# RWKV projections on Trainium2: K's product moved to the head of each tile, the low-rank products behind it

## What is computed

```python
xx = token_shift(hn) - hn
xs = hn[None] + xx[None] * mu[:, None, None, :]
r, k, v, g = jnp.einsum('pbsd,pdf->pbsf', xs[:4], w_in)
xv, xw, xa = xs[2], xs[4], xs[5]
w_log = -jax.nn.softplus(-(w0 + jnp.tanh(xw @ w1) @ w2)) - 0.5
a = jax.nn.sigmoid(a0 + (xa @ a1) @ a2)
```

## Time and profile before

| | us |
|---|---|
| median of 3 runs | 4384.56 |
| lowest, highest | 4382.27, 4392.83 |
| profiled execution: its own time | 4379.64 |
| profiled execution: span | 4377.9 |
| TensorE busy | 4071.0 (93%) |
| VectorE, ScalarE busy | 1501.9 (34%), 1254.9 (29%) |
| granted TensorE clock, mean | 0.968 |

### The profile page before, as it was taken

How to read it: one execution, slowest core, us unless ns; L and a number is a source line. 1 busy time by engine, 2 the same in 40 slices (tenths; PEclk the granted TensorE clock), 3 DMA queues, 4 the chain that set the end, 5 groups by cost and what they waited for, 6 DMA issues and landing times. The chain is left out here.

```text
span 4377.9 us, 70847 instructions
## 1 busy us (share of the span) xinstructions
PE 4071.0 (93%) x30130; PEld 2388.2 (55%) x30130; DVE 1501.9 (34%) x3325; ACT 1254.9 (29%) x2197; POOL 320.8 (7%) x143
## 2 busy tenths in 40 slices
PE   8999999989899999998999998998999879889798
PEld 3458844445466666544554455444444378788343
DVE  3346611132144444112331053103322176766111
ACT  1147700022255555201220054112222222221132
POOL 0000000000000000000000000000000046654000
PEclk9999999999999999998999999999999999999899
DMA  5000042042400100202002011014111121110300
GB/s 208 20 23 2 2 173 82 5 127 75 151 23 23 45 23 23 82 10 106 14 10 96 15 40 58 0 38 164 48 48 48 71 81 53 59 65 28 144 19 19
DMA packets 162429, 254.03 MB, mean 58 GB/s; under 512 B 48500, under 2 KB 92772, under 8 KB 162150
## 3 DMA queue, kind: packets, MB, share of 16 engines
q1 hardware_dynamic: 162152, 249.96, 16.2%
HBM read 187.36 MB, written 62.57 MB: 57 GB/s over the span
## 5 line engine op out<-in xcount | busy, mean ns | idle before, releaser
L1530 DVE TENSOR_SCALAR_CACHE_REDUCE la_s<-psum 128x512 f32<-128x512 f32 (+1 forms) x384 | 210.5, 598 | 298.8 <-PE psum L1597 298.8
L2569 POOL TENSOR_TENSOR rs_kk<-rs_k,rs_k_k 128x1024 f32<-128x1024 f32 x7 | 16.6, 2365 | 3644.0 <-DVE rs_k L2913 3522.6
L237 PE MATMUL psum<-retention_w,even_hT 128*128 128x512 f32 x544 | 238.8, 600 | 7.8 <-PEq L112 6.2
L1504 ACT ACTIVATE la_pT<-psum 128x512 f32<-128x512 f32 x320 | 177.1, 596 | 236.9 <-PE psum L1606 236.9
L237 PE MATMUL psum<-retention_w,rp_mixed 128*128 128x512 f32 x512 | 223.2, 594 | 3.0 <-DVE rp_mixed L2434 3.0
L237 PE MATMUL psum<-rp_w_last,rp_mixed 128*128 128x512 f32 x512 | 222.2, 592 | 0.0
L1591 PE MATMUL psum<-la_kT,la_qT 64*128 64x512 f32 (+1 forms) x768 | 166.1, 550 | 19.8 <-DMA la_v<-latent_v 14.6
L1496 ACT ACTIVATE la_s<-la_s,la_negm 128x1280 f32<-128x1280 f32 x128 | 175.2, 1368 | 24.8 <-DVE la_negm L1539 24.8
L1606 PE MATMUL psum<-ident,la_s 128*128 128x128 f32 x1280 | 180.4, 280 | 2.0 <-ACT la_pT L1504 1.9
L237 PEld LDWEIGHTS psum<-retention_w,even_hT 128*128 128x128 f32 x544 | 104.0, 193 | 136.5 <-issue 135.8
L1617 PE MATMUL psum<-la_pT,la_v 128*64 128x128 f32 x2560 | 167.8, 278 | 0.6 <-issue 0.6
(11 more groups left out here) (420 smaller groups left out, 7222.7 us busy)
## 6 DMA issues: line engine op xcount, KB each, us to landing
rwkv_raw<-x_rows SPq DMA_DIRECT2D x48, 512.0 KB, 2.6
later_slots<-in_ada_w_dram SPq DMA_DIRECT2D x16, 1024.0 KB
retention_w<-in_even_w_in_dram SPq DMA_DIRECT2D x8, 2048.0 KB, 12.6
ada_slots<-in_ada_w_dram SPq DMA_DIRECT2D x4, 2048.0 KB, 13.0
retention_w<-in_odd_w_in_dram SPq DMA_DIRECT2D x4, 2048.0 KB, 12.4
rp_w_last<-in_odd_w_in_dram SPq DMA_DIRECT2D x2, 4096.0 KB, 25.8
latent_v<-lp_v SPq DMA_DIRECT2D x10, 512.0 KB, 2.6
la_kT<-latent_kT SPq DMA_DIRECT2D x8, 640.0 KB, 5.6
```

Source lines behind the costliest of these rows:

```text
L237: last = pe.matmul(out[:, c:c + w], left[:, k, :], right[:, k, c:c + w], start=(k == 0), stop=(k == kd - 1))
L1504: act.activation(pT[:, h, at * BANK:(at + 1) * BANK], pT_banks[f % 2], ACT.Copy).then_inc(pT_moved[f % 2], 1)
L1530: dve.tensor_scalar(s_sb[:, g % 2, j, cols], s_banks[j][:, 0:cols.stop - cols.start], SCALE, NEG, ALU.mult, ALU.max, accum_out=smax[:, g % ...
L2569: eng.tensor_tensor(kk[:, :], k[s][:, :], k_k[:, :], ALU.mult).then_inc(q["kk_made"], 1)
```

## The change

The order of the streams becomes K, W, A, R, V, G, and that of the outputs K, W, R, A, V, G. On TensorE a tile is now K, W down, A down, W up, R, A up, V, transposes, G. ScalarE moves K's output before it makes the two hidden rows. VectorE mixes W while K's product runs, waits for K's product before it mixes A, and waits for the two down products before R's and V's. No instruction is added or removed.

```diff
-    ORDER = (W, A, K, R, V, G)
-    OUTPUTS = (K, A, R, W, V, G)
+    ORDER = (K, W, A, R, V, G)
+    OUTPUTS = (K, W, R, A, V, G)
...
                 def tile(i, ahead):
-                    act.wait_ge(down_made, i * 2 + 1)
-                    act.wait_ge(out_made, i * STREAMS)
-                    act.activation(hidden[0:LO, 0, :], down_banks[0], ACT.Tanh).then_inc(down_moved, 1)
-                    act.wait_ge(down_made, i * 2 + 2)
-                    act.activation(hidden[0:LO, 1, :], down_banks[1], ACT.Copy).then_inc(down_moved, 1)
                     for m, n in enumerate(OUTPUTS):
+                        if m == 1:
+                            act.wait_ge(down_made, i * 2 + 1)
+                            act.wait_ge(out_made, i * STREAMS)
+                            act.activation(hidden[0:LO, 0, :], down_banks[0], ACT.Tanh).then_inc(down_moved, 1)
+                            act.wait_ge(down_made, i * 2 + 2)
+                            act.activation(hidden[0:LO, 1, :], down_banks[1], ACT.Copy).then_inc(down_moved, 1)
                         act.wait_ge(out_made, i * STREAMS + (m + 1))
...
                     dve.wait_ge(out_made, i * STREAMS)
                     mix(i, 1)
-                    for j in (2, 3):
-                        dve.wait_ge(down_made, i * 2 + (j - 1))
+                    dve.wait_ge(out_made, i * STREAMS + 1)
+                    mix(i, 2)
+                    for j in (3, 4):
+                        dve.wait_ge(down_made, i * 2 + (j - 2))
                         mix(i, j)
-                    dve.wait_ge(out_made, i * STREAMS + 1)
-                    mix(i, 4)
...
                     first_product(i, 0)
                     first_product(i, 1)
                     first_product(i, 2)
+                    second_product(i, W)
+                    first_product(i, 3)
                     second_product(i, A)
-                    first_product(i, 3)
-                    second_product(i, W)
                     first_product(i, 4)
```

## The result

| | before | after |
|---|---|---|
| median of 15 runs, us | 4384.56 | 4396.6 |
| lowest to highest | 4371.0 to 4393.34 | 4383.47 to 4404.36 |
| profiled execution, span | 4377.9 | 4381.7 |
| TensorE busy | 4071.0 | 4070.4 |
| mean granted clock | 0.968 | 0.969 |

The ratio of the runs is 1.0027, with a 95% interval of 1.0017 to 1.0038: 12 us slower, between 7 and 17. 4396.6 lies inside the range of 4380 to 4403, and inside the 0.3% either way; the size of the loss was told too small.

What follows compares the result with a forecast made beforehand. TensorE's own work was taken as the bound, plus two buffers that come free late. Seven tile boundaries (4.8 us) and tile 0 (0.9) add 5.7 us to 4384.56, giving 4390 us, range 4380 to 4403.

Steps and rivals of the forecast that it cites:

- K starts at 3103.72, 1.18 us later: Tile's head: K waits for ScalarE to move G's output, starting 1.18 us later than W's down product did.
- W's and A's down products: Behind K: W's follows without a gap at 3117.64; A's waits 0.69 us for its mixture, starting at 3120.29.
- W's up product: Behind A's down product: starts 1.80 us after it, fills the former 0.43 us gap, hands on after 1.72.
- the 0.68 us: Start of R's product, 3123.81 instead of 3123.13: 0.68 us more per tile, 4.8 over seven tile boundaries.
- Tile 0: First tile, no G ahead, slow clock at the start: A's wait behind K is added, +0.9 us.
- Before the change K stood behind two down products, and the wait was covered: Old order: the wait for G's output cost K nothing; at the tile's head nothing covers it.
- Rival 1: ScalarE, between K's evacuation and tanh: tanh late, perhaps by a second table load; 10.5 us more, 4395; 6%.
- The drain: Tanh's table load: by the skill's rule tanh ends 1.38 us later, sum 10.5 us; forecast went by the trace's 0.01 gap.
- Rival 2: Every tile's start: TensorE's idle moments make the clock fall, seven losses totalling 18 us, 4408; 3%.
- Rival 3: Ahead of K: G's evacuation is not really paid for, so 8.3 us go, 4382; 4%.
- The sum: Whole kernel: 4.8 us for seven tile boundaries plus 0.9 for the first tile, 5.7 us more.

Runs made afterwards that it cites:

- the narrowed count: Changed kernel, but K's product waits only for V's output of the tile before, not for G's: ratio 0.9993 (0.9981 to 1.0005).
- cover runs: Kernel before, with a wait for G's output added at the loop's end, then in W's down product instead: 4401.48 and 4397.81 us, timed once each.
- the three comparisons: The changed kernel, unaltered, compared three times with the kernel before: ratios 1.0027, 1.0008 and 1.0018.

## Why the prediction was right

- *"K starts at 3103.72, 1.18 us later"*: right in place and nearly in size. From G's start to K's is 15.10 us, where the forecast had 15.01 (G at 3088.71 in the kernel before, K at 3103.72). The hand-over from ScalarE took 0.14 us (3101.68 + 1.02 to 3102.84), not the 0.06 of the earlier trace rows. The run with the narrowed count showed this wait to be the cause.
- *W's and A's down products*: 13.91 and 2.64 us after K's and W's start, forecast 13.92 and 2.65. The gap moved and kept its 0.69 us.
- *W's up product*: 1.89 us after A's down product starts, forecast 1.80 with bounds of 1.7 and 2.4; and it handed on after 1.83 us, where I took 1.72 from an up product behind a full one. These two and the hand-over are the terms that were mis-sized. They are 0.09, 0.11 and 0.09 short; the two down products' terms were 0.02 long. So the 0.68 us becomes 0.95, and the periods give 0.94. None of it shows as a gap. The extra time stands beside a down product, not wherever shapes change: in the earlier trace rows a full product hands on to an up product after 13.74 us and to the transposes after 13.73, but to a down product after 13.82, and an up product hands on after 1.72 behind a full product, but after 1.83 here.
- *Tile 0*: +1.1 us, forecast +0.9; the 0.09 and 0.11 of W's up product are missing here too. The clock was at 0.50 for some 5.5 us from TensorE's start, as in the earlier trace rows, though K's product now ran in it. Over ten profiles, some with K and some with W at the head, this stretch was between 5.3 and 5.9 us.
- *"Before the change K stood behind two down products, and the wait was covered"*: right for K there, whose wait of 1.2 us was shorter than the 3.7 us of the two down products. It does not mean that the old order hides any wait at its head. The two cover runs showed that a late start of W's down product itself has a price.
- *Rival 1* (tanh late) fell: there is one table load, not two, and tanh is 1.9 us early. The forecast itself had the load behind K's evacuation; it came ahead of it, as this rival had it, and delayed nothing that TensorE waited for.
- *The drain*: K's evacuation starts 0.01 us after the load ends, and the tile's next load starts 0.02 us after the row before it (3121.39 + 0.27 to 3121.68). The drain that the Trainium skill, "ScalarE: Activation LUTs", What ACT_TABLE_LOAD costs, adds to every switch of table set does not show in this trace.
- *Rival 2* (the clock) fell: 1.00 in tiles 1 to 7, with a gap of 1.2 us in each. The swing of the clock that the Trainium skill, "TensorE: Matmul & The Clock Gate", "A second HAM failure mode: psum-queue depth-cycling", tells of for frequent idle moments did not come here, with one such gap in 65 us.
- *Rival 3* fell: the wait is paid in full.
- *The sum*: 5.7 us against 7.7 in the stage and 12, 3.5 and 8 us in the three comparisons. That the median of 4396.6 lay within the range, with a sum 2 us short and a draw some 4 us high, it owes to the room that the range left for rival 1, which fell, and for the spread of the runs.

## What to carry to other kernels

Moving a product to the head of a loop makes it pay for whatever its first wait counts: look at what a clamped or rounded count asks for there, and at what stood in front to hide it. When two orders leave the same buffer late, ask for the buffer first; with one more, the order did not matter here. And where a reordering gives a short product other neighbours, add the times from one start to the next for those very neighbours: here they differed by about 0.1 us beside a down product, where no gap showed, and by nothing at the other changes of shape.

## What was not expected of the hardware

A wait on an empty instruction ahead of the loop's branch idled TensorE 1.81 us, the same count waited for on the first product behind the branch 1.21. The same form at the same place cost nothing when its count had long been reached: with the narrowed count K starts 13.74 us after G. So it seems that the branch is covered only if TensorE can take it while it still has work; but whether the branch or the empty instruction takes the 0.6 us was not tested. And the part behind the stage, untouched, differed between profiles by up to 20 us (885.5 to 906.1), and with it the granted clock (1.00 and 0.92 in the windows above). That is more than twice what the change is worth; only the stage's own length, which repeated to 0.15 us, could tell the parts of this change apart.
